# Attention on one core: values weighed in four groups of two, three, three and two key tiles instead of five pairs

## What is computed

```python
s = jnp.einsum('bkgqd,bksd->bkgqs', qb, k) * scale      # A: 8 query heads, 2 key heads, width 64
p = jax.nn.softmax(s, axis=-1)
o = jnp.einsum('bkgqs,bksd->bkgqd', p, v)
a = softmax(q1 @ k1) - lam * softmax(q2 @ k2)            # B: 4 heads, halves of width 32
o = a @ v
```

## Time and profile before

| | |
|---|---|
| median of 3 runs | 2335.69 us (2333.5 to 2337.78) |
| profiled execution | 2338.74 us, span 2336.9 us, mean granted TensorE clock 0.948 |
| busy: PE, DVE, ACT, POOL | 90%, 59%, 37%, 42% of the span |
| attention of the first layer | about 531 to 1026 us |
| attention of the second layer | up to about 2192 us |

### The profile page before, as it was taken

One profiled execution on the slowest core, in us unless ns is written; L12 is line 12 of the kernel. 1 busy time (PEld: TensorE's weight loads), 2 busy tenths in 40 slices (PEclk: granted clock), 3 DMA queues, 4 the chain that ended last, 5 costly groups with the idle time before them and its releaser, 6 DMA issues. The chain is left out here.

```text
span 2336.9 us, 28577 instructions
## 1 busy us (share of the span) xinstructions
PE 2104.8 (90%) x10517; PEld 1477.0 (63%) x10517; DVE 1369.1 (59%) x2298; ACT 855.1 (37%) x1760; POOL 979.4 (42%) x522
## 2 busy tenths in 40 slices
PE   3799999898999999959838999998899999999598
PEld 1678898665555555537716788886565555555276
DVE  1668300396777777787516672004957777777874
ACT  1432221433555555432123322214235554555321
POOL 0211111233778788760002111113348887887500
PEclk8999999899999999979969999998979999999799
DMA  7332221201011110024373322211011111110243
GB/s 273 104 122 87 73 64 59 47 2 42 20 19 26 26 19 19 14 77 139 108 267 108 113 91 64 71 58 42 3 41 19 21 25 29 23 19 8 98 119 108
DMA packets 188756, 155.74 MB, mean 67 GB/s; under 512 B 125180, under 2 KB 150208, under 8 KB 186560
## 3 DMA queue, kind: packets, MB, share of 16 engines
q1 hardware_dynamic: 185424, 153.35, 21.8%
q10 hardware_dynamic: 3184, 0.47, 0.1%
HBM read 115.37 MB, written 38.42 MB: 66 GB/s over the span
## 5 line engine op out<-in xcount | busy, mean ns | idle before, releaser
L1152 POOL TENSOR_TENSOR prob_sums<-prob_sums,probs 128x1024 f32<-128x1024 f32 x256 | 615.1, 2403 | 85.1 <-ACT probs L1311 56.3
L1311 ACT ACTIVATE probs<-scores 128x512 f32<-128x512 f32 x672 | 361.2, 603 | 378.0 <-PE scores L1210 162.4
L501 POOL TENSOR_TENSOR w_lo<-w_stage,w_hi 128x512 fp32r<-128x512 f32 (+1 forms) x112 | 134.3, 1232 | 823.8 <-ACT w_hi L436 823.8
L1377 DVE TENSOR_REDUCE neg_max_parts<-work 128x1 f32<-128x512 f32 (+1 forms) x640 | 395.7, 685 | 66.3 <-PE work L1190 60.9
L403 PE MATMUL z_acc<-w_hi,h_hi 128*128 128x512 f32 (+1 forms) x640 | 238.0, 372 | 14.4 <-DVE h_lo L520 8.9
L403 PE MATMUL z_acc<-w_lo,h_hi 128*128 128x512 f32 (+1 forms) x640 | 234.7, 367 | 0.0
L403 PE MATMUL z_acc<-w_hi,h_lo 128*128 128x512 f32 (+1 forms) x640 | 234.3, 366 | 0.0
L825 DVE MEMSET k_stackB<- 128x24 f32 (+1 forms) x4 | 0.9, 218 | 346.6 <-PEq L287 346.6
L1409 DVE RECIPROCAL recip_sums<-work 128x512 f32<-128x512 f32 x32 | 107.4, 3358 | 152.2 <-PE work L1242 152.2
L403 PE MATMUL z_acc<-h_hi,w_lo 128*128 128x512 f32 (+1 forms) x528 | 187.0, 354 | 0.0
L403 PE MATMUL z_acc<-h_hi,w_hi 128*128 128x512 f32 (+1 forms) x528 | 186.9, 354 | 0.0
(11 more groups left out here) (240 smaller groups left out, 3737.1 us busy)
## 6 DMA issues: line engine op xcount, KB each, us to landing
w_stage<-in_w_in SPq DMA_DIRECT2D x96, 256.0 KB, 3.0
mod_w<-in_w_mod SPq DMA_DIRECT2D x16, 1024.0 KB, 14.0
z_scratch<-z_out SPq DMA_DIRECT2D x60, 256.0 KB, 2.0
cv<-u_scratch SPq DMA_DIRECT2D x20, 512.0 KB, 6.3
mod_w<-in_w_mod SPq DMA_DIRECT2D x16, 512.0 KB, 21.4
u_scratch<-z_out SPq DMA_DIRECT2D x32, 256.0 KB, 2.0
out_y_sample<-y_tiles SPq DMA_DIRECT2D x16, 512.0 KB, 5.1
q_rawA<-z_scratch SPq DMA_DIRECT2D x16, 320.0 KB, 4.1
```

The lines of the kernel that those rows point to most:

```text
L501: pool.tensor_tensor(w_lo[:, n % RING, 0:cols], stage[:, n % STAGES, 0:cols], w_hi[:, n % RING, 0:cols].bitcast(F32), ALU.subtract).then_i ...
L1152: ins = pool.tensor_tensor(a, a, pr[:, n % NPB, :], ALU.add)
L1311: act.activation(pr[:, n % NPB, c * NB:(c + 1) * NB], sc[m % SCORE_BANKS][:, :], ACT.Exp, scale=SCALE[u]).then_inc(s["a_exp"], 1)
L1377: dve.tensor_reduce(dst, src, AX_X, ALU.max, negate=True).then_inc(s["a_wkdve"], 1)
```

## The change

Tiles 2 to 7 are weighed in two groups of three instead of three of two. The pieces 6 to 26, which lay in three intervals of 7, lie in two of 10 and 11. The scores of tile 4 come in the first interval, those of 5, 6 and 7 in the second, of 8 and 9 in the third. There are seven probability buffers instead of six. Nothing else changes; the amount of computation is the same.

```diff
-GROUPS = ((0, 1), (2, 3), (4, 5), (6, 7), (8, 9))
+GROUPS = ((0, 1), (2, 3, 4), (5, 6, 7), (8, 9))
...
-NPB = 6
+NPB = 7
...
-SLOTS = (((0, 2), (2, 2), (4, 2)), ((6, 2), (8, 3), (11, 2)), ((13, 2), (15, 3), (18, 2)), ((20, 2), (22, 3), (25, 2)))
+SLOTS = (((0, 2), (2, 2), (4, 1), (5, 1)), ((6, 2), (8, 3), (11, 3), (14, 2)), ((16, 4), (20, 4), (24, 3)))
```

## The result

| | before | after |
|---|---|---|
| median | 2336.12 us (2333.5 to 2337.78, 4 runs) | 2414.57 us (2409.17 to 2417.68, 4 runs) |
| span of the profiled execution | 2336.9 us | 2415.7 us |
| mean granted TensorE clock | 0.948 | 0.942 |

The ratio is 1.0336, with a 95% interval of 1.0323 to 1.0348: the change makes the kernel 78.5 us slower. 2405 us was forecast, with a range of 2362 to 2424.

The account below looks back on a forecast made before the run. TensorE, busy 90% of the span, was taken as the bound, with VectorE and POOL right behind in B units. Terms summed to 34.5 us per layer, 69 in two: 2408 profiled, 2405 us median, range 2362 to 2424.

Parts of the forecast that it names:

- One group fewer: In all 32 units: one weighing group and two borders saved on TensorE, 0.35 us each, 11.2 us if nothing else waits.
- right behind TensorE: In B units: VectorE's maxima and POOL's adds end just behind TensorE's work, and the change moves work toward both.
- the sign of the whole: Whole kernel: slower by over 0.2%, chance 0.90; forecast 3.0% slower.
- The four work banks: Last two piece intervals: piece k waits for maximum k-4, so later pieces start 0.60 us apart; last interval 5.32 us.
- The rival that only the banks wait: Loads land without delay and ScalarE has slack: A +0.39, B +1.26 us a unit, 2362 us; chance 0.20, shared with no late loads.
- The split and its late load: Middle interval: tile 7's second half waits for ScalarE's split and its later load; interval 6.62 us in A, 5.8 in B.
- The A chain: A unit's middle interval: load issued 620.08, lands 4.1 us later, split 1.35, then chunk 15; interval 6.62 us.
- The B interval: B unit's middle interval: load lands 3.2 us after issue, split 1.6, weighing at 654.5; interval 5.8 us.
- The A term: Ordinary A units: 18.38 us against 16.64 over the compared stretch, +1.74 us each.
- the units with new A keys: Longer load and three casts split: +4.2 us for that A unit, +4.9 for the B unit after it, per layer.
- the clock falls as well: Rival: TensorE's clock drops after the four long waits, 1.6 to 3 us each, about +9, 2414 us; chance 0.08.
- +0.6 as in any B unit: B unit's first interval: tile 4's two score matmuls (0.46 us) and about 0.14 for borders, +0.6 us.

Follow-up runs that it names:

- the kernel built to be that case: The changed kernel with ScalarE's split of the unit two ahead moved from behind tile 5 to behind tile 7: 2358.43 us, ratio 1.0103.

## Why the prediction was right, and what was mis-sized

**One group fewer, 0.35 us: shown.** A units of 30.03 instead of 30.38 in every kernel whose piece intervals have no wait. In B units POOL's adds take it away, which the prediction had as "right behind TensorE" and had not carried through to this term; with the sign of the whole it made no difference.

**The four work banks: shown.** The last interval was forecast at 5.32 us in both kinds and measured 5.30 in both, the middle one of an A unit by the banks alone at 5.27 and measured 5.27. A simple count (a piece after the fourth starts 0.60 us after the one before) gave these to a few hundredths. The rival that only the banks wait gave 2362 us, and the kernel built to be that case took 2358.43.

**The split and its late load: shown.** The A chain, in the prediction's own steps: load issued 0.52 us before the interval, 0.53 measured; landed 4.1 after, 4.02; split 1.35, 1.26; interval 6.62, 6.53. The B interval was 5.49 instead of 5.8, mainly because the load landed 2.96 us after its issue and not 3.2 (ScalarE, kernel after, issue at 653.81):

```profile
656.77 0.92 ACT L1325 CAST k_stackB<-k_rawB 128x384 fp32r<-128x384 f32 x2 [0.25 <-DMA q_rawB<-z_scratch]
...
915.18 0.93 ACT L1325 CAST k_stackB<-k_rawB 128x384 fp32r<-128x384 f32 x2 [1.18 <-DMA q_rawB<-z_scratch]
```

A quiet B unit is therefore +1.9 to +2.0 and not +2.4. The means of 2.68 and 2.34 come mainly from two units in each layer where a load landed later, as in the second row: issued at 911.30, it was waited for until 915.18, 3.88 us, and that unit is +4.47. The A term is alike: quiet units are near +1.55 and not +1.74, and the second layer's mean of 2.01 holds one unit of +3.97, whose load was issued and landed late. So the means of both terms came out near the forecast by luck: the quiet case was put too high, and single late loads, two of them with a fall of the clock (below), made up for it. Moving the load away or the split away returned 49 and 56 of the 78 us. They are two halves of one wait, not two costs to be added.

**The term that was too small: the units with new A keys.** Forecast +4.2 and +4.9, measured +6.7 to +7.1 and +6.4 to +9.0. Their long waits were there, but for the B unit of the second layer. TensorE, kernel after, first in the A unit and then in the B unit after it, both in the first layer, and last in a later B unit:

```profile
754.77 0.79 PE L1209 MATMUL scores<-qTA,kTA 128*128 128x512 f32 x1 [3.77 <-ACT probs L1311]
...
756.77 4.71 PE L1226 MATMUL att_out<-probs,vA 128*64 128x512 f32 x12
...
792.66 0.80 PE L1212 MATMUL scores<-qT2B,kTB 128*128 128x512 f32 x1 [2.69 <-ACT probs L1311]
...
794.24 4.76 PE L1226 MATMUL att_out<-probs,vB 128*64 128x512 f32 x12
...
917.37 0.54 PE L1212 MATMUL scores<-qT2B,kTB 128*128 128x512 f32 x1 [1.73 <-ACT probs L1311]
...
918.69 3.97 PE L1226 MATMUL att_out<-probs,vB 128*64 128x512 f32 x12
```

Twelve matmuls of a group take 2.79 us elsewhere. After idle stretches of 3.77, 2.69 and 1.73 us they take 4.71, 4.76 and 3.97. The window over the first of them, kernel after, columns as in the earlier trace rows:

```profile
755.00:760.00 5.00, 5.00 (x12) 1.93 (x14) 1.29 (x2) 1.29 (x3) 4.58 (x2) 0.50 0.00 0
```

The granted clock is 0.50, the 1.2 GHz level, while TensorE is busy all the time. From the start of the middle interval to the end of its weighing this A unit took 14.82 us (746.60 to 761.42) against 9.26 in an ordinary one (624.70 to 633.96), 5.56 more: 2.77 by the longer wait (3.77 against 1.00), and 2.79 in matmuls that ran slower. For the B unit it is 12.76 (786.16 to 798.92) against 8.22: 4.54 more, 1.89 by the wait and 2.65 by the rest. So the rival "the clock falls as well" came true in part. It had priced exactly this, 1.6 to 3 us for each of the four long waits, about +9 and 2414 us, which is nearer to the measured 2414.57 than the forecast is, and was given 8 in 100. The forecast took the long waits and left their clock out, though the earlier trace rows show it after an idle stretch. The ordinary waits, 1.00 and 0.80 us, left the clock at full rate, as the forecast had it.

In the second layer the A unit waited 3.98 us, but the B unit only 1.24, and its weighing behind that took 2.79. Its +6.41 us lie mostly in its first interval, where the forecast had +0.6 as in any B unit. From the unit's first scores to its piece 6 the kernel before took 9.40 us in both layers; now it is 13.42 (1979.35 to 1992.77), and 11.91 in the first layer (774.25 to 786.16). ScalarE copies the new keys there, and the scores of tile 4, which the change put into this interval, wait for it. TensorE, kernel after, second layer:

```profile
1986.40 0.79 PE L1212 MATMUL scores<-qT2B,kTB 128*128 128x512 f32 x1 [0.76 <-ACT probs L1311]
...
1989.21 3.63 PE L1226 MATMUL att_out<-probs,vB 128*64 128x512 f32 x8
```

The eight weighing matmuls took 1.92 us at this place in the kernel before. The granted clock was 0.71 from 1984 to 1989 us and 0.61 from 1989 to 1994.

Units with nearly equal waits, one with the clock held and one without, show what the clock costs by itself. In the kernel after, the B unit with the wait of 1.73 us above (917.37) is 31.15 us long; another waited 1.62 (720.32), its twelve weighing matmuls took 2.79 at a granted clock of 1.00 (716 to 726 us, against 0.83 in 914 to 924), and it is 29.42 long. In the kernel with the late split, the B unit after new A keys has the same waits in both layers:

```profile
764.06 0.50 PE L1213 MATMUL scores<-qT2B,kTB 128*128 128x512 f32 x1 [0.76 <-ACT probs L1312]
...
766.07 3.09 PE L1227 MATMUL att_out<-probs,vB 128*64 128x512 f32 x8
...
1938.13 0.50 PE L1213 MATMUL scores<-qT2B,kTB 128*128 128x512 f32 x1 [0.76 <-ACT probs L1312]
...
1939.65 1.89 PE L1227 MATMUL att_out<-probs,vB 128*64 128x512 f32 x8
```

It is 32.36 us long in the first layer and 30.66 in the second; 1.7 us are the clock alone. So moving the split took the long waits away, but not every fall of the clock. What no run here has is one of the waits near 3 us or longer with the clock held, so in the units above the division into wait and clock is read from rows of one execution.

**Where the 78.5 us went.** Taking the split away from the middle interval returns 56 us, of which about 49 go with the load's lateness and the clock that it costs, and 7.5 with the split's place. The other 22 are mostly the four work banks: 0.30 us in each A unit, 1.12 in each ordinary B unit, net of the group saved; the B units after new A keys hold more, 3.83 and 2.12, in part by the clock. Easing the piece intervals returns these and 3 us more.

## What to carry to other kernels

Merging two steps of the bounding engine saves their border, but it also joins the intervals between them, and an interval is where other engines catch up: count, for the longer interval, what each ring of buffers allows (here 0.60 us a piece past the fourth) and what in-order work of another engine now falls inside it. When an item in such a queue waits for a load, ask what issues the load, and whether the change moves that too; either cure, an earlier issue or a later use, returned most of the loss. And different kinds of unit may want different orders: the gain was in the A units alone, because in the B units another engine was the bound.

## What the hardware showed unexpectedly

Idle stretches of TensorE well below 2 us, in the middle of a busy phase, were followed by slow matmuls, but not each time. In the kernel after, stretches of 1.43, 1.52, 1.68 and 1.73 us (1801.54, 596.82, 2151.95, 917.37) were followed by weighing at 3.86, 3.69, 4.49 and 3.97 us instead of 2.79; those of 1.56, 1.62 and 1.76 us (2119.55, 720.32, 1925.33), and the ordinary ones of 1.00 and 0.80, by full rate. Two short ones, 0.65 and 0.76 us, were followed by a granted clock of 0.66 (780 to 785 us). So the length of one stretch does not tell it. A long wait cost about twice its length: in the A unit above, 2.77 us more of waiting came with 2.79 us of slower matmuls. Over the middle of the first layer the mean granted clock fell from 1.00 to 0.97, and it was 1.00 again in both kernels that took the wait away. Windows over 556 to 980 us, kernel after:

```profile
556.00:980.00 424.00, 398.42 (x1949) 230.24 (x1948) 280.00 (x414) 200.04 (x393) 310.16 (x141) 0.97 0.10 19
```
